# Gate columns beside the identity in the transposing products, and scatter in blocks of three, in an expert-mixture decoder kernel

## The reference

```python
def hier_moe(h, w_grp, b_grp, w_exp, b_exp, w_gate, w_up, w_down):
    ...                                     # softmax over 4 groups, then over the 8 experts of the best one
    top_p, top_i = lax.top_k(pe, TOP_K)     # TOP_K = 2
    gate = pg_sel * top_p / jnp.sum(top_p, axis=-1, keepdims=True)
    expert_id = g_sel[:, None].astype(jnp.int32) * EXPERTS_PER_GROUP + top_i.astype(jnp.int32)
    ...                                     # tokens sorted by expert into blocks
    def expert_block(args):
        xb, e = args
        return (jax.nn.silu(xb @ w_gate[e]) * (xb @ w_up[e])) @ w_down[e]
    ...
    y = y_buf[dest] * g_flat[order][:, None].astype(h.dtype)
    out = jnp.zeros((T, D), h.dtype).at[token_idx].add(y)
```

## Time and profile before

| | |
|---|---|
| median of 3 runs | 1904.9 us (1904.06 to 1905.84) |
| profiled execution, its own time | 1904.18 us |
| its span, first to last instruction | 1902.4 us |
| PE, PE weight loads | 1863.3 us, 925.6 us busy |
| DVE, ACT, POOL | 586.9, 368.7, 160.7 us busy |
| scatter products (L681, yhi and ylo) | 216.1 us busy |
| gate products (L668) | 17.7 us busy, 128 of them |
| transposing products (L707) | 18.3 us busy, 128 of them |
| granted TensorE clock, mean | 0.991 |

### The profile page before, as it was taken

One profiled execution on the slowest core, in us unless ns is written; L12 is line 12 of the kernel. 1 busy time (PEld: TensorE's weight loads), 2 busy tenths in 40 slices (PEclk: granted clock), 3 DMA queues, 4 the chain that ended last, 5 costly groups with the idle time before them and its releaser, 6 DMA issues.

```text
span 1902.4 us, 18477 instructions
## 1 busy us (share of the span) xinstructions
PE 1863.3 (98%) x7588; PEld 925.6 (49%) x7588; DVE 586.9 (31%) x1111; ACT 368.7 (19%) x623; POOL 160.7 (8%) x152
## 2 busy tenths in 40 slices
PE   8999999998999999999999999999999999999997
PEld 5445644545445454544444444455454444444443
DVE  3999211224122222221222322213322222222223
ACT  2433211212111110111124231122211111111112
POOL 0556110010000000000020000100100000000001
PEclk9999999998999999999999999999989999999998
DMA  9214422202999999999961211302169999999992
GB/s 361 97 40 164 160 89 89 83 10 105 413 405 406 412 405 415 403 415 404 371 226 44 89 44 45 132 1 92 55 262 415 403 412 408 414 405 414 405 413 117
DMA packets 90602, 477.55 MB, mean 251 GB/s; under 512 B 7759, under 2 KB 8189, under 8 KB 40973
## 3 DMA queue, kind: packets, MB, share of 16 engines
q1 hardware_dynamic: 89164, 470.88, 61.8%
q0 software_dynamic: 736, 3.15, 0.6%
q10 hardware_dynamic: 608, 2.24, 0.3%
HBM read 472.05 MB, written 4.19 MB: 250 GB/s over the span
## 4 chain that ended last, share of the span: by engine, by line
PE 90%; DVE 7%; issue 1%; DMA 1%; ACT 0%; POOL 0%; POOLq 0%; SPq 0%; DVEq 0%; ACTq 0%
PE PS L628 24%; PE PS L443 17%; PE PS L656 11%; PE PS L399 11%; PE PS L681 7%; PE PS L698 7%; DVE PS L1854 5%; PE PS L967 3%; PE PS L461 2%; PE PS L541 1%; PE PS L450 1%; PE PS L688 1%; PE PS L642 1%; PE PS L707 1%; PE PS L668 1%
## 5 line engine op out<-in xcount | busy, mean ns | idle before, releaser
L443 PE MATMUL PS<-hT,ring 128*128 128x512 f32 x640 | 277.7, 593 | 1.9 <-DVE xT L1728 1.2
L628 PE MATMUL PS<-ring,hT 128*64 128x512 f32 x1024 | 226.4, 595 | 1.3 <-DVE small L1719 1.3
L628 PE MATMUL PS<-ring,xg 128*64 128x512 f32 x1024 | 226.8, 595 | 0.0
L1728 DVE TENSOR_TENSOR xT<-PS,xT 128x512 f32<-128x512 f32 x256 | 158.6, 681 | 217.0 <-PE PS L681 217.0
L656 PE MATMUL PS<-ring,hT 128*64 128x512 f32 x960 | 212.6, 595 | 1.4 <-ACT hT L1324 1.4
L443 PEld LDWEIGHTS PS<-hT,ring 128*128 128x128 f32 x640 | 120.9, 190 | 149.9 <-issue 148.6
L628 PEld LDWEIGHTS PS<-ring,hT 128*64 128x64 f32 x1024 | 74.0, 137 | 132.8 <-issue 131.1
L628 PEld LDWEIGHTS PS<-ring,xg 128*64 128x64 f32 x1024 | 72.6, 137 | 132.2 <-issue 132.0
L1755 DVE TENSOR_TENSOR ylo<-PS,yhi 128x1024 fp32r<-128x1024 f32 (+1 forms) x32 | 38.1, 1191 | 294.1 <-ACT yhi L1330 285.1
L656 PEld LDWEIGHTS PS<-ring,hT 128*64 128x64 f32 x960 | 66.3, 137 | 125.4 <-issue 119.9
L681 PE MATMUL PS<-onehotT,yhi 128*128 128x512 f32 x256 | 114.9, 449 | 1.1 <-DVE xT L1728 1.1
(11 more groups left out here) (282 smaller groups left out, 1746.6 us busy)
## 6 DMA issues: line engine op xcount, KB each, us to landing
ring<-in_moe_w_gate SPq DMA_DIRECT2D x128, 1024.0 KB, 11.2
ring<-in_moe_w_up SPq DMA_DIRECT2D x128, 1024.0 KB, 12.1
ring<-in_moe_w_down SPq DMA_DIRECT2D x128, 1024.0 KB, 9.2
ring<-in_xa_w_kv SPq DMA_DIRECT2D x16, 1024.0 KB, 7.4
ring<-in_gla_w_in SPq DMA_DIRECT2D x12, 1024.0 KB, 13.1
ring<-in_conv_w_in SPq DMA_DIRECT2D x8, 1024.0 KB, 14.8
ring<-in_xa_w_q SPq DMA_DIRECT2D x8, 1024.0 KB, 6.3
ring<-in_xa_w_o SPq DMA_DIRECT2D x8, 1024.0 KB, 6.8
```

What stands on the lines that cost most here:

```text
L443: mm = pe.matmul(bank(b), w[:, k * 512 + m * P:k * 512 + (m + 1) * P], src[:, k, :], start=(k == 0), stop=(k == C - 1))
L628: mm = pe.matmul(PS[e * SL:(e + 1) * SL, kind * BANK:(kind + 1) * BANK], x[:, k, (2 * (p % 2) + e) * SL:(2 * (p % 2) + e + 1) * SL], ring[ ...
L1728: dve.tensor_tensor(xT[:, c, :], bank(XBANK + b), xT[:, c, :], ALU.add).then_inc(g[f"x_read{b}"], 1)
```

## The change

Three things are changed in the experts' stage, and the positions of some tiles in SBUF move with them.

1. The separate gate products go. A tile `comb` holds, twice, 6 gate columns, the 128 columns of the identity and 6 more gate columns. `one_hot_T` multiplies each of its four weight tiles by 134 columns of it, identity and gates, in two bank uses (`hot_unit`) of two tiles each; in a bank the six gate columns in the middle add up over both tiles. DVE fills the gate columns of the next pair (`gates_beside`), sums the two banks' parts and adds them (`take_gates`); ACT copies the transposed part in two halves (`one_hot_taken`).
2. The group is moved: the one of pair `p + 1` now ends pair `p` (the one of pair 0 stands behind the opening gathers), and `onehotT` has two buffers. PE's wait for the transposed one-hot ahead of the scatter goes.
3. The scatter runs in blocks of 3, 3 and 2 chunks instead of 4 and 4; the third block stands behind the first gather, in the last two pairs behind the transposes. `unit` numbers the uses accordingly. DVE adds three chunks before the hidden rows and five after them, and builds the next quad's one-hot behind the gates instead of ahead of them.

```diff
             if p == -1:
                 n = k - 8
             elif p == 0:
-                n = 4 if k == 0 else k - 4
+                n = 5 if k == 0 else k - 3
             elif p < NP - 2:
-                n = 12 * p - 4 + k
+                n = 12 * p - 3 + {7: 8, 8: 9, 9: 7}.get(k, k)
             elif p == NP - 2:
-                n = 12 * p - 4 + min(k, 9)
+                n = 12 * p - 3 + min(k, 9)
             else:
-                n = 12 * p - 6 + min(k, 9) if p < NP else 12 * p - 9 + k
+                n = 12 * p - 5 + k if p < NP else 12 * p - 9 + k
             return n % 3, PER_ROUND * r + n // 3
+
+        def hot_unit(p, i):
+            return (p, 0) if i else (p - 1, 11) if p else (-1, 12)
...
-                def gates(p):
-                    ...
                 def scatter(p, cs):
                     if cs[0] == 0:
                         pe.wait_ge(g["ylo_done"], YS * r + p)
-                        taken(p - 1, 11)
...
                 def one_hot_T(p):
-                    b, done = use(p, 11)
                     q, s = p // 2, p % 2
-                    for t in range(TT):
-                        mm = pe.matmul(bank(b, t * P, (t + 1) * P), onehot[:, q % 2, t, s * P:(s + 1) * P],
-                                       identR[:, :], start=True, stop=True)
-                    mm.then_inc(done, 1)
+                    pe.wait_ge(g["comb_ready"], 2 * (NP * r + p + 1))
+                    for i in range(2):
+                        b, done = use(*hot_unit(p, i))
+                        for j in range(2):
+                            mm = pe.matmul(bank(b, j * P, j * P + P + 6),
+                                           onehot[:, q % 2, 2 * i + j, s * P:(s + 1) * P],
+                                           comb[:, i, 6:P + 12] if j == 0 else comb[:, i, 0:P + 6],
+                                           start=(j == 0), stop=(j == 1), skip_group_check=True)
+                        mm.then_inc(done, 1)
...
                 for p in range(NP):
-                    gates(p)
                     if s == 0:
-                        for k in ((8, 9, 10, 11) if p == 0 else (9, 10)):
+                        for k in ((9, 10, 11) if p == 0 else (10,)):
                             taken(p - 1, k)
...
                     up(p, 0, "gate_full")
                     if p:
-                        scatter(p, range(0, 4))
+                        scatter(p, range(0, 3))
                     up(p, 1, "up_full")
                     if p:
-                        scatter(p, range(4, 8))
+                        scatter(p, range(3, 6))
                     transposed(p)
                     if more:
                         ...
                         gather(q + 1, p, 9, 4 * s)
+                    if p:
+                        scatter(p, range(6, 8))
                     if p < NP - 1:
                         down(p)
                         if more:
                             gather(q + 1, p, 10, 4 * s + 2)
-                        one_hot_T(p)
+                        one_hot_T(p + 1)
                     else:
...
                         down_half(p, 0)
-                        one_hot_T(p)
                         down_half(p, 1)
...
+                def one_hot_taken(p):
+                    for i in range(2):
+                        b, n = unit(r, *hot_unit(p, i))
+                        act.wait_ge(g["gates_in"], 2 * (NP * r + p) + i + 1)
+                        act.wait_ge(g[f"x_full{b}"], n + 1)
+                        act.activation(onehotT[p % 2][:, i * 2 * P:(i + 1) * 2 * P].rearrange("p (j s) -> p j s", j=2),
+                                       bank(XBANK + b, 0, 2 * (P + 6)).rearrange("p (j s) -> p j s", j=2)[:, :, 0:P],
+                                       ACT.Copy).then_inc(g[f"x_read{b}"], 1)
...
                 def take_gates(p):
...
+                    for i in range(2):
+                        b, n = unit(r, *hot_unit(p, i))
+                        dve.wait_ge(g[f"x_full{b}"], n + 1)
+                        dve.tensor_reduce(gsums[i], bank(XBANK + b, P, P + 6).rearrange("p (h v) -> p v h", h=2), AX.X,
+                                          ALU.add).then_inc(g["gates_in"], 1)
+                    dve.wait_ge(g["gates_in"], 2 * (NP * r + p + 1))
+                    for v, dst, rows in ((2, rslot, slice(0, P)), (0, gcol[0:SL, :], slice(0, SL)),
+                                         (1, gcol[SL:, :], slice(SL, P))):
+                        dve.tensor_tensor(dst, gsums[0][rows, v:v + 1], gsums[1][rows, v:v + 1], ALU.add
+                                          ).then_inc(g["gates_ready"], 1)
+                    dve.wait_ge(g["gates_ready"], 3 * (NP * r + p + 1))
+
+                def gates_beside(p):
+                    q, s = p // 2, p % 2
+                    for j, cols in enumerate((slice(P + 6, P + 12), slice(0, 6))):
+                        dve.tensor_copy(comb[:, :, cols], gtab[:, q, j:TT:2, s, :]).then_inc(g["comb_ready"], 1)
```

74 lines of the change are left out of this document (31 added, 43 removed).

## The result

| | before | changed |
|---|---|---|
| median | 1905.2 us (4 runs, 1904.06 to 1905.84) | **1879.9 us** (4 runs, 1878.65 to 1885.36) |
| ratio | | 0.9874, 95% interval 0.9861 to 0.9886 |
| profiled execution, its span | 1904.18 us, 1902.4 us | 1885.36 us, 1883.6 us |
| busy DVE, ACT | 586.9, 368.7 us | 608.8, 371.4 us |

The forecast was 1881.7 us, in a range of 1879.0 to 1889.5. The median came 1.8 us under it. The profiled execution is the slowest of the four, 5.5 us above the median, and that needs an explanation of its own (the first and the last of the experiments).

What follows compares the result with a forecast made beforehand. PE was taken as the bound, a chain of start-to-start steps. Savings of 6.2 + 0.4 + 11.6 + 3.5 + 1.5 = 23.2 us bring 1904.2 to 1881.0, with the median 0.7 higher: 1881.7 us, range 1879 to 1889.5.

Steps and rivals of the forecast that it cites:

- Part A: Pair boundaries: dropping the gate products saves 0.39 us at odd ones (6.2 us), 0.03 at even ones (0.4 us).
- rival 3: Merged products no cheaper, costing a scatter product's 0.24 us instead of about 0.11: 15.4 us back, 1897 us; 3%.
- Part B: Scatter in blocks of three: no bank waits for DVE's additions, 0.385 us a pair in 30 pairs, 11.6 us.
- covers: Slack before PE would wait: 0.3 us at the first gather's bank, 0.3 at the transposes, 1 at the third block.
- part C: Last two pairs of a layer: two scatter chunks fill PE's 0.88 us wait for the hidden rows' copy, 3.5 us.
- D: Last pair of a layer: transposing group leaves the gap between the down halves, 0.74 us each, 1.5 us in all.
- floor of 29.8 us: Weight stream: transferring a pair's 12.6 MB alone would need 29.8 us, under the 30.24 us expected on average.
- store: Weight stream's time in hand: half an up tile lands some 15 us before its next use.
- Rivals 1: Even boundaries lose 0.25 us instead of gaining 0.03 (+3.9 us), third block pays its entry (+2.6): 1888.2 us; 24%.
- 2: Weight stream binds, queues cannot use the idle 1.0 us and have no store; gain taken back, 1904.9 us; 3%.
- 4: DVE late for the bank of the pair's first gather, behind the transposes; 1.4 us late gives 1910 us; 2%.
- 5: Even boundaries give 0.39 us too, since ACT's copy starts earlier than now: 1876.6 us; 3%.

Runs made afterwards that it cites:

- the first and the last of the experiments: First: the changed kernel again, no edit, 1880.8 us. Last: the changed kernel with PE's branch-announcing mark after pair 15 instead of 13, 1882.9 us.
- clean profile: Profile of the unedited changed kernel run again, without the added first-layer stall: span 1878.5 us; that run's median 1880.8 us.
- the mark after pair 13 or 8: Place of PE's branch announcement: 13 as before, 8 earlier. Changed kernel 1879.9 and 1880.8 us (13), 1880.3 (8); second gather moved ahead 1875.8 and 1876.6 (13), 1875.2 (8).
- the kernel with the early gather: Changed kernel with a pair's second gather ahead of the down stream instead of behind it: 1875.8 us, ratio 0.9848; again 1876.6 us.
- the light kernel: Changed kernel without the scatter's second products (ylo, the low part of the expert outputs), to see the weight stream bind: 1867.9 us, one run.

## Why the prediction was right

- **The bound and the pair lengths.** 30.06 and 30.42 us were forecast, 30.06 and 30.41 came, in 13 of the 16 pairs of each layer (1 to 13; the first and the last two have a chain of their own). The chain's saving, 23.12 us, is the sum of 23.2.
- **Part A.** 0.39 us at odd and 0.03 at even boundaries are both shown, by the rows of after and by putting the products back. The hand-over from ACT took 0.05 us, as in the earlier trace rows. The Trainium skill's floor for small products was not reached. The opening of a layer kept its 0.33 us behind ACT's copy, as the earlier trace rows had it, and what it hangs on stays open. The merged products' 134 columns cost nothing (0.59 us for four at 915.44, as with 128 in the earlier trace rows), so rival 3 is out.
- **Part B.** All bank waits of the ordinary pairs are gone. The covers that were put at 0.3 us for the first gather and for the transposes held (the hidden rows are done at 573.62, the transposes' load begins at 573.95), and the third block's entry cost nothing. Alone it gave, with part C, 14.8 of 15.1 us.
- **Parts C and D.** The two chunks fill the gap of the hidden rows' copy, and the last down stream is unbroken (934.66 to 941.68, 7.02 us).
- **The added work.** DVE's 22 us more are hidden wholly. The prediction let DVE's changes cost nothing, and missed that they could also gain: DVE begins its first addition 0.1 us earlier. It changes no time here, because part B removes the wait that it would have shortened.
- **The weight stream.** The floor of 29.8 us was right to 0.01 us, by the experiment that reaches it. The store was mis-sized, 10.8 and 11.7 us instead of some 15, which changes no time of the changed kernel, since its pairs stay over the floor.
- **Rivals 1, 2, 4, 5.** None came true. Rival 5's boundaries can be had, but only with the gather moved, and then they give 0.33 us each.
- **Outside the pairs.** Here is what the sum left out. "Nothing outside the pairs is touched on PE" is true of the instructions and false of the time: in the clean profile the first layer's opening lost 1.0 us, with a clock that rose later, the second's won 0.4, the end won 1.5 where ACT's gap had been, and PE's branch took 0 or 4.8 us. That the sum came so near is luck in this part: the clean profile nets 0.8 us of gain that nobody had reckoned with, and the two executions at 1878.7 us, which pull the median 1.8 us below the forecast, left no trace. The spread of 1 us in the range was too small: the four times of the changed kernel lie within 6.7 us, and nine of the kernel before, taken beside it in the first round of experiments, within 4.0.

## What to carry to other kernels

Where one engine is the bound without a gap, cost an edit by the steps from start to start of its instructions, and ask at every place what else releases the next one: the same four products were worth 0.39 us at one boundary and 0.03 at the next. Small products that load their own weights are best hidden as extra columns of products that load the same weights anyway, and results that rotate through three buffers go in runs of three. Parts of a change that shorten the same wait don't add up, so measure each by itself and the whole, and look at the branch at a stage's end before you trust a single execution.

## What the runs showed that I had not expected

- PE's conditional branch took 3.61 us in one execution and 0.49 in another of the same program, and in every first-layer case of over 3 us the granted clock fell behind it (0.67 over the next 8 us here), which cost 2.7 us more. In the 22 branches with the mark after pair 13 or 8, the long ones are those that had no transfer of PE's instructions begun in the 33 us ahead of them.
- Moving the announcement of that branch from two pairs ahead to none cost 3.5 to 4.3 us in the kernel with the early gather, although no instruction that computes moves. In the changed kernel the difference is within the spread.
- A wait for a transfer can stand under "issue" in the row of the weight load and under its name only in the row of the product beside it; the light kernel's 1.82 us at the up stream is one.
